# Recurrent scan: the products of a block inverse alternate between two partition layouts, so that each uses four 64x64 tiles of the array

## What is computed

```
S  = S * decay + (S @ a) b^T + v k^T        (a state of 64x64)
y  = S @ r
```

## Time and profile before

| | |
|---|---|
| median of 3 executions | 3834.08 us (3832.83 to 3836.97) |
| span of the profiled execution | 3830.5 us |
| TensorE busy in the span | 3423.5 us (89%) |
| VectorE, ScalarE, GpSimd busy | 1710.6, 978.6, 40.7 us |
| first scan of `decays` to its last (12 steps) | 236.7 to 555.0 us |
| last product of the inverse begins | 608.1 us |

### The profile page before, as it was taken

One profiled execution on the slowest core, in us unless ns is written; L12 is line 12 of the kernel. 1 busy time (PEld: TensorE's weight loads), 2 busy tenths in 40 slices (PEclk: granted clock), 3 DMA queues, 4 the chain that ended last, 5 costly groups with the idle time before them and its releaser, 6 DMA issues. The chain is left out here.

```text
span 3830.5 us, 66346 instructions
## 1 busy us (share of the span) xinstructions
PE 3423.5 (89%) x28910; PEld 2722.6 (71%) x28910; DVE 1710.6 (45%) x2845; ACT 978.6 (26%) x1671; POOL 40.7 (1%) x48
## 2 busy tenths in 40 slices
PE   5969997997998899996989977899999978979998
PEld 3848995766867666654845845788887867868877
DVE  3655554563245211114545347544443356555643
ACT  2135441242222111112011143311112132533322
POOL 0000000000000000001000000000000000000000
PEclk8969997998998899997999988999999989999999
DMA  6130002603355699995521101144432111013332
GB/s 243 61 138 4 4 4 92 191 30 98 97 171 206 263 422 424 423 423 189 177 92 50 56 13 34 56 117 128 120 108 72 61 39 42 1 51 98 94 108 85
DMA packets 254322, 486.84 MB, mean 127 GB/s; under 512 B 12394, under 2 KB 148107, under 8 KB 245364
## 3 DMA queue, kind: packets, MB, share of 16 engines
q1 hardware_dynamic: 246964, 457.91, 34.1%
q0 software_dynamic: 1984, 16.81, 1.2%
q10 hardware_dynamic: 5120, 8.39, 0.6%
HBM read 453.68 MB, written 29.39 MB: 126 GB/s over the span
## 5 line engine op out<-in xcount | busy, mean ns | idle before, releaser
L398 PE MATMUL banks<-leading,w_rest 128*128 128x512 f32 (+2 forms) x2016 | 733.6, 364 | 60.8 <-DVE w_rest L335 60.4
L398 PE MATMUL banks<-rest,w_leading 128*128 128x512 f32 (+2 forms) x2016 | 722.7, 358 | 0.0
L398 PE MATMUL banks<-leading,w_leading 128*128 128x512 f32 (+2 forms) x2016 | 721.0, 358 | 0.0
L335 DVE TENSOR_TENSOR w_rest<-land,w_leading 128x1024 fp32r<-128x1024 f32 (+2 forms) x344 | 321.7, 977 | 516.6 <-ACT w_leading L320 516.6
L398 PEld LDWEIGHTS banks<-leading,w_rest 128*128 128x128 f32 (+1 forms) x2016 | 383.3, 190 | 133.4 <-DVE w_rest L335 40.9
L320 ACT CAST w_leading<-land 128x1024 fp32r<-128x1024 f32 (+2 forms) x344 | 275.7, 850 | 711.2 <-DMA land<-in_w_in 246.2
L398 PEld LDWEIGHTS banks<-leading,w_leading 128*128 128x128 f32 (+1 forms) x2016 | 383.0, 190 | 57.6
L398 PEld LDWEIGHTS banks<-rest,w_leading 128*128 128x128 f32 (+1 forms) x2016 | 384.0, 190 | 53.7
L398 PE MATMUL banks<-w_rest,leading 128*128 128x512 f32 (+3 forms) x772 | 297.3, 385 | 51.6 <-DVE w_rest L335 51.6
L398 PE MATMUL banks<-w_leading,rest 128*128 128x512 f32 (+3 forms) x772 | 292.0, 378 | 0.0
L398 PE MATMUL banks<-w_leading,leading 128*128 128x512 f32 (+3 forms) x772 | 290.9, 377 | 0.0
(11 more groups left out here) (586 smaller groups left out, 5050.5 us busy)
## 6 DMA issues: line engine op xcount, KB each, us to landing
wg<-in_w_exp_gate SPq DMA_DIRECT2D x32, 2048.0 KB, 24.8
wu<-in_w_exp_up SPq DMA_DIRECT2D x32, 2048.0 KB, 26.8
wd<-in_w_exp_down SPq DMA_DIRECT2D x32, 2048.0 KB, 25.3
ws<-in_ada_w SPq DMA_DIRECT2D x96, 512.0 KB, 3.8
land<-in_w_in SPq DMA_DIRECT2D x41, 1024.0 KB, 5.5
land<-in_ffn_up SPq DMA_DIRECT2D x44, 512.0 KB, 5.4
land<-in_ffn_up SPq DMA_DIRECT2D x88, 256.0 KB, 3.3
ws<-in_w_ada SPq DMA_DIRECT2D x32, 512.0 KB, 3.8
```

The lines of the kernel that those rows point to most:

```text
L335: nc.vector.tensor_tensor(rest[s % 2][:, k0:k1, 0:n], slots[s % wslots][:, k0:k1, 0:n], leading[s % 2][:, k0:k1, 0:n].bitcast(F32), ALU.su ...
L398: mm = nc.tensor.matmul(bank_of(r, kind, at), lhsT, rhs, start=(k == 0 and q == 0), stop=(k == kt - 1 and q == len(each) - 1))
```

## The change

The 14 products per tile stay 14, but 13 of them become `turned_product`. It takes chunk `c` on the row group `c` and puts a result on the column group of the head's half, so the four combinations of row and column group occur in turn. A result then stands in another layout: the partitions hold the head's half, and the chunk is where the half was. The next product turns it back. Matrices of both layouts can't meet in one product, so the factors are regrouped: `(I + D)(I + D^4)` and `(I + D^2)(I + D^8)` are each made in one layout and then multiplied, and the last products are taken as `(I + M^2) T` and `(I + M)` times that.

A turned product writes to banks 0 and 1 together (one per row group), in the half `at`. So both products of a pair must be complete before ScalarE reads either half, where it could before copy bank 0 during the product in bank 1.

The sums with the unit matrix move: three are made by GpSimd from copies in SBUF (`with_eye`), two by VectorE out of PSUM (`result_with_eye`). VectorE has 4 steps per tile on results where it had 5, ScalarE 10 copies where it had 9. The transposing product with the unit matrix (L1675) goes. The last product moves from behind `carry_state` and `y_state` to before them.

The core of the diff:

```diff
+            def turned_product(at, lhsT, rhs):
+                for p in range(4):
+                    for rows, out in ((0, 0), (1, 1), (0, 1), (1, 0)):
+                        mm = nc.tensor.matmul(m.ps[C(out), rows, 256 * at + p * CH:256 * at + (p + 1) * CH], lhsT[C(rows), 2 * p + out, :], rhs[C(rows), 2 * p + out, :],
+                                              start=True, stop=True)
+                mm.then_inc(inv_made_sem, 1)
...
-                        pe.wait_ge(inv_added_sem, 5 * j - 1)
-                    product(0, b.DT, b.D)
-                    product(1, b.D, b.DT)
+                        pe.wait_ge(inv_added_sem, added)
+                    turned_product(0, b.DT, b.D)
+                    turned_product(1, b.D, b.DT)
...
-                    pe.wait_ge(inv_copied_sem, 9 * j + 2)
-                    pe.wait_ge(et_new_sem, j + 1)
-                    product(0, b.D2T, b.D2)
-                    product(1, b.D2, b.D2T)
...
-                    product(2, b.D2, et)
+                    pe.wait_ge(inv_copied_sem, copied + 2)
+                    turned_product(0, b.D2T, b.D2)
+                    turned_product(1, b.D2, b.D2T)
                     rest_turn(j)
-                    pe.wait_ge(inv_copied_sem, 9 * j + 4)
-                    product(0, b.D4T, b.D4)
-                    pe.wait_ge(inv_added_sem, 5 * j + 1)
-                    product(2, b.D4, et)
+                    pe.wait_ge(inv_copied_sem, copied + 4)
+                    turned_product(0, b.D4T, b.D4)
                 if last:
                     gq(j - 1, 0)
                     carry_rows(j - 1, 0)
                 if now:
-                    pe.wait_ge(inv_added_sem, 5 * j + 2)
-                    product(1, b.D8, et)
+                    pe.wait_ge(eyed_sem, eyed + 2)
+                    pe.wait_ge(inv_added_sem, added + 1)
+                    turned_product(0, et, D4_eye)
                 if last:
                     gq(j - 1, 1)
                 if now:
-                    pe.wait_ge(inv_added_sem, 5 * j + 3)
...
+                    product(2, D8_eye, second_eye)
+                    pe.wait_ge(inv_copied_sem, copied + 6)
+                    turned_product(0, high_and_second, low_and_fourth)
+                    turned_product(1, low_and_fourth, high_and_second)
                 if new:
                     k12(j + 1)
                 if last:
                     carry_state(j - 1, 0)
                 if now:
-                    product(0, b.NT, E_)
-                    product(1, E_, b.NT)
+                    pe.wait_ge(inv_copied_sem, copied + 7)
+                    pe.wait_ge(inv_added_sem, added + 2)
+                    turned_product(0, b.NT, T16)
+                    turned_product(1, T16, b.NT)
                 if last and lat(j - 1):
                     y_inner(j - 1)
                 if now:
-                    pe.wait_ge(inv_copied_sem, 9 * j + 8)
-                    product(0, MT_, M_)
+                    pe.wait_ge(inv_copied_sem, copied + 9)
+                    turned_product(0, MT_, M_)
...
-                    product(1, M2_, et)
+                    pe.wait_ge(inv_added_sem, added + 3)
+                    turned_product(0, M2_eye, TT16)
                 if j + 2 < RW_TILES:
                     gates(j + 2)
+                if now:
+                    pe.wait_ge(inv_copied_sem, copied + 10)
+                    pe.wait_ge(eyed_sem, eyed + 3)
+                    turned_product(0, M_eye, Y_)
                 if last:
                     carry_state(j - 1, 1)
                     if lat(j - 1):
                         y_state(j - 1, 1)
-                if now:
-                    product(2, M_, Y_)
                 if new and lat(j + 1):
                     k5(j + 1)
...
-            def copy_result(j, made, dst, bank):
+            def copy_result(j, made, dst, at):
                 act.wait_ge(inv_made_sem, 14 * j + made)
-                nc.scalar.copy(dst[:, :, :], heads(m.ps[:, bank, :])).then_inc(inv_copied_sem, 1)
+                nc.scalar.copy(by_half(dst[:, :, :]), by_rows(at)).then_inc(inv_copied_sem, 1)
...
+            def with_eye(dst, x):
+                nc.gpsimd.tensor_tensor(dst[:, :, :], x[:, :, :], eye, ALU.add).then_inc(eyed_sem, 1)
...
+            for j in range(RW_TILES):
+                pool.wait_ge(inv_copied_sem, COPIES * j + 2)
+                with_eye(b.ET[(j + 1) % 2], b.D2T)
+                pool.wait_ge(inv_copied_sem, COPIES * j + 3)
+                pool.wait_ge(z_made_sem, j + 1)
+                with_eye(D4_eye, b.D4)
+                if j + 1 < RW_TILES and lat(j + 1):
+                    bonus(j + 1)
+                pool.wait_ge(inv_copied_sem, COPIES * j + 8)
+                with_eye(M_eye, M_)
```

More of the change, by code:

```diff
@@ L1461, in rwkv_scan, with by_rows @@
             gated_sem, exps_made_sem, rows_copied_sem, z_copied_sem, inv_copied_sem, ua_copied_sem, y_copied_sem, coef_copied_sem,
-            run_sem, pre_sem, rows_new_sem, wc_new_sem, rt_new_sem, d_new_sem, akt_new_sem, rb_new_sem, et_new_sem, inv_added_sem, gt_new_sem, qt_new_sem, s_new_sem, y_added_sem, coef_added_sem,
+            eyed_sem, run_sem, pre_sem, rows_new_sem, wc_new_sem, rt_new_sem, d_new_sem, akt_new_sem, rb_new_sem, et_new_sem, inv_added_sem, gt_new_sem, qt_new_sem, s_new_sem, y_added_sem, coef_added_sem,
             bonus_sem, chain_sem):
-        E_, M_, MT_, M2_, Y_ = b.D8, b.D2, b.D2T, b.D4, b.D4T
+        low_and_fourth, high_and_second = b.D, b.DT
+        T16, M_, MT_, TT16, M2_eye = b.D2, b.D2T, b.D4T, b.D4, b.D2
+        D4_eye, D8_eye, M_eye = b.AKT, b.D8, b.D8
+        COPIES, ADDS, EYES = 10, 4, 3
+        def by_rows(at):
+            return m.ps[:, 0:2, 256 * at:256 * (at + 1)].rearrange("q a (p e) -> q a p e", e=CH)
         def y_free(eng, j):
@@ L1671, in _ @@
                 if now:
-                    pe.wait_ge(inv_added_sem, 5 * j + 3)
[L1673 to L1676, removed]
+                    if lat(j):
+                        coef_free(pe, j)
+                    product(2, D8_eye, second_eye)
+                    pe.wait_ge(inv_copied_sem, copied + 6)
+                    turned_product(0, high_and_second, low_and_fourth)
+                    turned_product(1, low_and_fourth, high_and_second)
                 if new:
@@ L1746, in _ @@
                 if now:
[L1747 removed]
+                    copy_result(j, 2, b.D2, 0)
                     copy_result(j, 2, b.D2T, 1)
@@ L1768, in _ @@
                     nc.scalar.copy(b.ZA[:, :, 0:CH], heads(m.ps[:, 7, :])).then_inc(z_copied_sem, 1)
-                    copy_result(j, 6, b.D8, 0)
-                    copy_result(j, 9, E_, 0)
-                    copy_result(j, 10, M_, 0)
+                    copy_result(j, 6, low_and_fourth, 0)
+                    act.wait_ge(inv_made_sem, 14 * j + 7)
+                    nc.scalar.copy(high_and_second[:, :, :], heads(m.ps[:, 2, :])).then_inc(inv_copied_sem, 1)
+                    copy_result(j, 9, T16, 0)
+                    copy_result(j, 11, M_, 0)
                     copy_result(j, 11, MT_, 1)
-                    copy_result(j, 12, M2_, 0)
+                    copy_result(j, 13, b.ET[j % 2], 0)
                 if new and lat(j + 1) and nth(j + 1) <= 4:
@@ L1786, in _, with bonus @@
         def _(pool):
-            for j in range(RW_FIRST_LAT, RW_TILES):
+            eye = m.cident[:, :].unsqueeze(1).to_broadcast([P, 8, CH])
+            def with_eye(dst, x):
+                nc.gpsimd.tensor_tensor(dst[:, :, :], x[:, :, :], eye, ALU.add).then_inc(eyed_sem, 1)
+            def bonus(j):
                 pool.wait_ge(rows_new_sem, 3 * (j + 1))
@@ L1900, in _ @@
                         nc.vector.tensor_tensor(b.QT[:, :, :, :], m.ps[:, 4, :].rearrange("q (c p e) -> q c p e", c=2, e=CH), rt, ALU.add).then_inc(qt_new_sem, 1)
+                if now:
+                    dve.wait_ge(inv_copied_sem, COPIES * j + 7)
+                    take_result(j, 9, TT16, 1)
                 if new and lat(j + 1):
@@ L1906, in _ @@
                     state(j - 1, 0)
+                if now:
+                    result_with_eye(j, 12, M2_eye, 0)
                 if new:
                     masks_k(j + 1)
-                if now:
-                    dve.wait_ge(inv_added_sem, 5 * j + 3)
-                    add_result(j, 13, et, Y_, 1)
-                if last:
-                    state(j - 1, 1)
                 if new and lat(j + 1) and nth(j + 1) > 4:
@@ L1920, in _ @@
                 if now:
-                    dve.wait_ge(inv_added_sem, 5 * j + 4)
-                    add_result(j, 14, Y_, b.TT, 2)
+                    take_result(j, 14, b.TT, 0)
+                if last:
+                    state(j - 1, 1)
                 if last and lat(j - 1) and nth(j - 1) > 4:
```

40 lines of the change are left out of this document (13 added, 27 removed).

## The result

| | median of the runs, us | ratio to before, 95% interval |
|---|---|---|
| before | 3835.5 (3832.8 to 3838.2) | |
| changed | 3811.0 (3807.9 to 3813.1) | 0.9941 (0.9927 to 0.9955) |

The change gives 24.5 us where 52.6 were forecast, and the time lies 5 us above the range. The kernel got faster, but by less than half of what was worked out.

The account below looks back on a forecast made before the run. TensorE's own work was taken to bound the scan. Shorter products less new waits gave 3 us in step 0, 4 x 4.2, 6 x 4.8 and 4 in step 11: 52.6 saved, 3834.1 to 3781.5 us, range 3766 to 3806.

Parts of the forecast that it names:

- Thirteen products per step save 6.0 us, 12 steps 71.8: Scan: each turned product takes 0.47 us instead of 0.93, saving 0.46, before new waits are taken off.
- Wait A: Before product 8, for ScalarE's copy of product 7: TensorE waits 1.26 us per step, 1.05 shown as idle.
- Wait B: Before `k5`, for ScalarE's sigmoids, in latent steps: 0.8 us idle where 0.35 stood, 0.45 more.
- The wait for `MT`: Before product 12 in steps 1 to 4: 0.5 us more, as both copies now start after product 11.
- C: Before product 10, for the copy of `T16` and then VectorE's of `TT16`: a new wait of 0.3 us.
- The transposing product's wait: TensorE's wait on VectorE before the transposing product, 0.62 us per step, would be removed.
- copies out of two banks: ScalarE's new copies, reading two banks by halves: 0.64 us each where others take 0.59.
- Rival 1: Scan: the new waits are twice those found, 26 us less gained, 3807 us; chance 10%.
- Rival 2: GpSimd's lock on VectorE reaches the path once per step, 15 us less gained, 3797 us; chance 5%.
- rival 3: The granted clock falls where TensorE now idles more; in six steps 20 us lost, 3802 us; chance 6%.
- Rival 4: The four tiles don't overlap in this order, products stay at 0.93 us, 3853 us, slower; chance 4%.
- rival 5: Most new waits are covered because later work slides into them, 3768 us; chance 3%.

Follow-up runs that it names:

- e7: Changed kernel plus 1,024 further matmuls without waits behind the last scan step, 512 of 64 columns, then 512 of 128: 3866.1 us, ratio 1.008.
- e8: Changed kernel with fewer, wider matmuls for the same columns in latent steps (UA times bt and RBT rows, kt times at and rt): 3794.9 us, ratio 0.9893.
- e9: Changed kernel run once more, unaltered, as a control: 3802.2 us, ratio 0.992 to the kernel before.
- e4: Changed kernel with product 7 moved ahead of the second part of `gq`, to cover the wait before product 8: 3805.3 us, ratio 0.9932.
- e3: Changed kernel without GpSimd's three sums with the unit matrix, so the inverse is another one: 3805.3 us, ratio 0.9921.
- e5: Changed kernel with half of the columns of `ua` left out, same number of TensorE instructions, output not the reference's: 3804.4 us, ratio 0.992.
- e11: Changed kernel with e8's wider matmuls and e4's order of product 7: 3796.4 us, ratio 0.99.

## Why the prediction was wrong

**The step that failed** is the first: "in the scan TensorE's own work sets the pace", and with it the term "Thirteen products per step save 6.0 us, 12 steps 71.8". A second bound lay just under the work. Before, 64 records of a product took 0.93 us, which is 3.72 a block and as long as a block took to arrive in e7 (3.75). At 0.47 a block of products would last about 2 us, and that speed can't be used. In the five intervals TensorE lost 25.7 us of work (152.3 to 126.7) and the time fell by 10.1. The row of before, to lay beside that of the changed kernel under e8:

```profile
396.80:555.00 158.20, 152.34 (x4852) 144.69 (x4850) 83.79 (x135) 76.84 (x147) 11.59 (x10) 1.00 0.02 4
```

The changed kernel's second median (e9), 3802.2 us, lies inside the range of 3766 to 3806 and 21 us above the forecast. That changes nothing in the step that failed: its five intervals are 146.1 us with 20.1 idle.

**The size fits.** Forecast were 47 us less between the first and the last `decays` scan, measured are 26.9. Pauses at multiples of 256 grew by 16.1 us between the two; 26.9 + 16.1 = 43.0. The 4 us that are left are small beside what such a sum can tell, as some waits would be longer without these pauses. No run took the fetch away altogether, so what the change would give without it stays an estimate.

**It could have been seen.** The earlier trace rows holds `[1.51 <-issue]` at 264.91, inside a product. I read it as idle time ahead of a fall of the clock. It lies at a multiple of 256, as do the six others counted above in the kernel before. The question left out was what TensorE waits for where it waits for nothing shown, and how near that is to binding once the work halves.

**Steps that held.** Products start 0.47 apart (0.47 forecast):

```profile
438.52 0.67 PE L1505 MATMUL banks<-D,DT 64*64 64x64 f32 x32
438.99 0.68 PE L1505 MATMUL banks<-DT,D 64*64 64x64 f32 x32
439.45 1.96 PE L1585 MATMUL banks<-ZA,TT 64*64 64x128 f32 x32
```

Wait A is there in all twelve steps, 8.3 / 12 = 0.69 idle where 1.05 stood in the sum. Wait B, ahead of `k5`, is 6.9 / 7 = 0.99 where 0.8 stood. The wait for `MT` in the early steps is 5.9 / 5 = 1.2 where it had been 0.68, as the forecast's 0.5 more said, and the first product of a step waits 0.6 for `TT` (1.8 us in 3), as forecast. C shows once, 0.5 us in the last step, where nothing of a next tile covers it. The transposing product's wait is gone. These terms were worth a few us either way.

**A term that was off, without weight:** copies out of two banks take 0.59, not 0.64:

```profile
443.59 0.58 ACT L1731 COPY D<-banks 128x512 f32<-128x512 f32 x1 [0.48 <-PE banks L1505]
444.07 0.59 ACT L1731 COPY D4T<-banks 128x512 f32<-128x512 f32 x1
```

**The rivals.** Rival 1, waits twice as large, comes nearest by its number (3807) and is wrong in kind: the waits are as I priced them, and cutting one gave nothing (e4). Rival 2, the lock, is refuted by e3. The Trainium skill's rule on the shared port (SBUF — State Buffer, the two separate sides) is borne out by 1.76 against 0.69; it cost nothing here, where the fetch set the pace. One of the forecast's signs of being wrong did appear, a wait of TensorE on GpSimd: 1.1 us, once, in step 0. The clock, rival 3, did not fall, from step 1 to the end of the scan:

```profile
270.40:581.10 310.70, 260.81 (x9931) 239.45 (x9923) 172.13 (x261) 162.43 (x317) 68.82 (x50) 1.00 0.02 4
```

Rival 4, no overlap of the tiles, falls with the 0.47, and rival 5, most waits covered, with waits A and B. The Trainium skill (TensorEngine Tiling, PSUM Bottleneck) says that the emptying of PSUM may become the bound. ScalarE is busy for 15.92 of 32 us, and no run bears that out here. The case that came true stood in no rival.

## What to carry to other kernels

Before making TensorE's instructions shorter, count them: 256 records (an fp32 matmul is four, two weight loads and two matmuls) took 3.5 to 4.0 us where nothing but their arrival held them up (e7), 15 ns a record. So 16 fp32 matmuls had about 0.95 us to fill, with 64 columns as with 128. Where pauses named `issue` lay a multiple of 256 records apart, fewer and wider instructions gained time in the latent steps (e8), and fewer columns, better cover of a wait or less work elsewhere didn't (e5, e4, e3). Compare the idle time of two kernels as well as the work: when it grows by as much as the work falls, look for the bound that is counted in something else.

## What the hardware showed that I had not expected

**TensorE's instructions arrive in blocks, and the arrival can set the pace**: 3.46 to 4.02 us a block where nothing else slows TensorE (e7). In its first half the spread goes with the packet's own 0.88 to 1.40 us. The Trainium skill (Runtime: NRT & Kernel Launch, Instruction fetch mechanics) describes the blocks: 256 instructions or 16 KiB, fetched by the sequencer through a DMA queue of its own while the block ahead is executed. By that section of the Trainium skill the cost of a boundary is mostly hidden. The trace agrees on the blocks and the queue (201 packets of 16 KB) and not on the cost: 20.0 us of pauses between the changed kernel's first `decays` scan and its last.

**Of GpSimd and VectorE, the one that begins later was lengthened, whichever it was.** A sum of GpSimd takes 1.26 us and `ET`, with both inputs in SBUF, 0.68. In one step GpSimd began first and kept its length; in the next `ET` did, by 0.05 us. (In one step, with starts 0.02 us apart by the trace, the earlier one, GpSimd, was lengthened.)

```profile
454.86 1.26 POOL L1801 TENSOR_TENSOR D<-D2T,cident 128x512 f32<-128x512 f32 x1 [2.81 <-ACT D2T L1731]
455.14 1.52 DVE L1877 TENSOR_TENSOR ET<-DT,cident 128x512 f32<-128x512 f32 x1
...
485.81 0.68 DVE L1877 TENSOR_TENSOR ET<-DT,cident 128x512 f32<-128x512 f32 x1
485.86 1.75 POOL L1801 TENSOR_TENSOR D<-D2T,cident 128x512 f32<-128x512 f32 x1 [4.69 <-ACT D2T L1731]
```

**Open:** four intervals of e8 ahead of the five, from the third scan to the seventh, took 3.2 us more than in the changed kernel (105.1 instead of 101.9). In e4 and e11 they took 4.4 and 4.8 more, and no run was made to find out why. Open too is why packets start when they do, which the records show and no run varied.
